# Differential attention on one core: where the heads' small PE work stands between the projection's half units, and how the second softmax map is scaled

## The reference

```
q, k = rmsnorm(q) * 64**-0.5, rmsnorm(k)             # per head two maps of 64 values
s    = einsum('bqhtd,bkhtd->bhtqk', q, k) + bias     # t = 0, 1: the two maps
pr   = softmax(s)                                    # over 512 keys
attn = pr[:, :, 0] - lam * pr[:, :, 1]
o    = rmsnorm(attn @ v) * (1 - lam_init)            # per head, 128 values, eps 1e-6
o    = o * silu(z);  out = o @ w_out
```

## Time and profile before

| what | value |
|---|---|
| median of three runs | 821.05 us |
| the profiled execution: time, span | 821.67 us, 819.9 us |
| PE busy in the span | 764.7 us, 93% |
| DVE, ACT, POOL busy | 503.3, 402.1, 451.8 us |
| chain that ended last | PE 49%, DVE 23%, issue 12%, ACT 7%, POOL 7% |
| head iterations 0 to 10 and the end | 488.7 to 819.9 us of the span |

### The profile page before, as it was taken

How to read it: one execution, slowest core, us unless ns; L and a number is a source line. 1 busy time by engine, 2 the same in 40 slices (tenths; PEclk the granted TensorE clock), 3 DMA queues, 4 the chain that set the end, 5 groups by cost and what they waited for, 6 DMA issues and landing times.

```text
span 819.9 us, 11592 instructions
## 1 busy us (share of the span) xinstructions
PE 764.7 (93%) x3856; PEld 616.5 (75%) x3856; DVE 503.3 (61%) x880; ACT 402.1 (49%) x806; POOL 451.8 (55%) x258
## 2 busy tenths in 40 slices
PE   4999999999999999997999999989999999998788
PEld 3777788878878787875878887767777777776566
DVE  4756858585848576773841131566867768678632
ACT  6447473728283745555531244264545554654510
POOL 5457574848484857564845326654553735536101
PEclk9999999999999999998999999999999999999898
DMA  8274464644637263534532224322313222220002
GB/s 252 79 217 103 160 148 154 155 155 111 198 76 206 76 167 114 154 155 102 180 105 84 78 77 126 114 70 68 100 53 100 74 76 75 69 82 26 0 1 102
DMA packets 100196, 91.10 MB, mean 111 GB/s; under 512 B 5456, under 2 KB 87728, under 8 KB 97080
## 3 DMA queue, kind: packets, MB, share of 16 engines
q1 hardware_dynamic: 95760, 66.99, 27.9%
q10 hardware_dynamic: 4264, 23.50, 9.4%
q0 software_dynamic: 128, 0.05, 0.0%
HBM read 88.13 MB, written 2.39 MB: 110 GB/s over the span
## 4 chain that ended last, share of the span: by engine, by line
PE 49%; DVE 23%; issue 12%; ACT 7%; POOL 7%; DMA 1%; DVEq 1%; ACTq 0%; SPq 0%; POOLq 0%
PE bank L1343 42%; DVE c_acc L995 6%; POOL w_lo L486 3%; DVE bank L1089 2%; ACT ex L835 2%; POOL stat L477 2%; PE bank L1420 2%; DVE sbias L1210 2%; DVE bank L1081 1%; DVE ex L1221 1%; ACT qkvz L900 1%; DVE tmp L1076 1%; ACT w_hi L621 1%; DVE stat L1214 1%; PE bank L1394 1%
## 5 line engine op out<-in xcount | busy, mean ns | idle before, releaser
L486 POOL TENSOR_TENSOR w_lo<-w_raw,w_hi 128x1024 fp32r<-128x1024 f32 x104 | 257.8, 2481 | 229.2 <-ACT w_hi L621 229.1
L1343 PE MATMUL bank<-hn_hi,w_hi 128*128 128x512 f32 (+1 forms) x392 | 157.3, 401 | 14.7 <-DVE BT L1010 11.7
L1343 PE MATMUL bank<-hn_hi,w_lo 128*128 128x512 f32 (+1 forms) x392 | 153.2, 391 | 0.0
L1343 PE MATMUL bank<-hn_lo,w_hi 128*128 128x512 f32 (+1 forms) x392 | 152.8, 390 | 0.0
L621 ACT CAST w_hi<-w_raw 128x1024 fp32r<-128x1024 f32 x104 | 108.7, 1047 | 72.1 <-PE bank L1343 68.4
L1343 PE MATMUL bank<-w_hi,hn_hi 128*128 128x512 f32 x320 | 131.4, 411 | 8.8 <-DVE zT L1010 6.1
L1343 PE MATMUL bank<-w_lo,hn_hi 128*128 128x512 f32 x320 | 125.9, 393 | 0.0
L1343 PE MATMUL bank<-w_hi,hn_lo 128*128 128x512 f32 x320 | 125.8, 393 | 0.0
L995 DVE SCALAR_TENSOR_TENSOR c_acc<-bank,par,c_acc 128x510 f32<-128x510 f32 (+1 forms) x128 | 95.8, 749 | 26.0 <-ACT c_acc L665 17.2
L835 ACT ACTIVATE ex<-sbias,stat 128x512 f32<-128x512 f32 x64 | 45.7, 716 | 120.5 <-DVE stat L1214 120.5
L1343 PEld LDWEIGHTS bank<-hn_hi,w_hi 128*128 128x128 f32 (+1 forms) x392 | 73.2, 187 | 33.1 <-issue 15.6
(11 more groups left out here) (191 smaller groups left out, 1231.9 us busy)
## 6 DMA issues: line engine op xcount, KB each, us to landing
w_raw<-in_ssd_w_in SPq DMA_DIRECT2D x48, 512.0 KB, 4.1
w_raw<-in_attn_w_in SPq DMA_DIRECT2D x64, 256.0 KB, 3.1
rows<-acs_rows ACTq DMA_DIRECT2D x14, 1024.0 KB, 6.0
edec<-exp_rows ACTq DMA_DIRECT2D x16, 512.0 KB, 6.3
w_raw<-in_ssd_w_out SPq DMA_DIRECT2D x16, 512.0 KB, 3.6
w_raw<-in_attn_w_out SPq DMA_DIRECT2D x16, 256.0 KB, 3.1
wbias<-bias_rows SPq DMA_DIRECT2D x8, 448.0 KB, 4.2
rows<-in_x SPq DMA_DIRECT2D x4, 512.0 KB, 5.2
```

The costliest lines, as they stand in the source:

```text
L486: nc.gpsimd.tensor_tensor(w_lo[:, s, :], w_raw[:, s, :], f32(w_hi[:, s, :]), ALU.subtract)\
L1343: ins = T.matmul(dst, a[i], b[j], start=first and n == 0, stop=last and n == 2)
```

## The change

The head steps of iterations 0 to 10 are put in another order on every engine, and one instruction changes its size:

- **PE.** Behind the even-numbered half units (the second, fourth, sixth and eighth, that is s = 1, 3, 5, 7) stand scores first, then the output's transposes or the values, then the transposes of the probabilities. Block 2 goes from s = 0 to 1, block 3 from 2 to 3, block 0 from 4 to 5, block 1 from 6 to 7. The transposes of q and k go from s = 3, where they stood ahead of `probs_t`, to s = 4, alone. Stages 0, 2 and 6 have no head step. In iterations 8 and 9 the fills go to (8; 1, 3, 4, 5, 7) and (9; 1).
- **ACT.** `exps` follow the scores to stages 1, 3, 5 and 7. In stage 1 and 3 `probs_hi` stands ahead of `exps`; in stage 5 the output's split and `probs_hi` do. In stage 7 the evacuation of the next head stands ahead of `exps`. v and z go from stage 1 to 2, the split of q and k from 3 to 4, behind that stage's `split_hi`.
- **DVE.** In the same manner; `biased` of block 1 and `combine` of block 1 both stand in stage 7, the gate in stage 6, the squares' reduction of the output in stage 3, its scaling in stage 4.
- **POOL.** The small `power` of the output goes from stage 2 (ahead of v's low part) to stage 3.
- **Arithmetic.** `combine` no longer divides map 0 by its sum: it works out one number per row, -lam times sum 0 over sum 1, and adds map 1 times that to map 0. The head's output is thereby larger by sum 0, and the RMS norm's epsilon is multiplied by the square of sum 0 (one more small instruction for each head). The 128x512 instruction L1221 becomes a 128x1 one.

Instructions of the PE, the exponentials, the transfers and all other sizes stay. Of the orders, the diff shows the lines as they stand after the change; those taken away stand in the listing above.

```diff
@@ -577,10 +578,10 @@
             pool.wait_ge(qk_ms, it)
             power(stat[:, 16:32], stat[:, 0:16], 4 * NC).then_inc(qk_rs, 1)
     par_ = (half + 1) % 2
+    if s == 3 and has(3):
+        pool.wait_ge(o_ms, it - 2)
+        power(stat[:, 52:56], stat[:, 48:52], NC).then_inc(o_rs, 1)
     if s == 2:
-        if has(3):
-            pool.wait_ge(o_ms, it - 2)
-            power(stat[:, 52:56], stat[:, 48:52], NC).then_inc(o_rs, 1)
...
@@ -827,13 +828,14 @@
 nc.scalar.activation(stat[:, 60:62], stat[:, 60:62], ACT.Exp).then_inc(sp_a, 1)
 act.wait_ge(h_rstd, 1)
-def exps(hd, q):
+def exps(hd, q, par_):
     act.wait_ge(smax, hd * NC + q + 1)
     after(act, a_done, hd * NC + q)
     for j in range(2):
+        total = SUM0 + par_ * NC + q if j == 0 else 41
         nc.scalar.activation(ex[:, j, :], sbias[:, j, :], ACT.Exp, bias=stat[:, 36 + j:37 + j],
-                             accum_out=stat[:, 40 + j:41 + j]).then_inc(e_done, 1)
+                             accum_out=stat[:, total:total + 1]).then_inc(e_done, 1)
...
@@ -843,64 +845,59 @@
 def stage_ops(m, half, s, has):
     it = m * 2 + 2 + half
+    one, two = (half + 1) % 2, half
+    if s == 0 and has(3):
+        act.wait_ge(pv_done, it - 2)
+        after(act, og_done, it - 3)
+        nc.scalar.copy(o_chan[:, :], bank[7][:, :]).then_inc(o_copied, 1)
+    if s == 1 and has(2):
+        probs_hi(it - 2, 1)
+        exps(it - 2, 2, two)
+    if s == 2:
         if has(1):
             act.wait_ge(qkvz_in, it * NC)
             after(act, pv_done, it - 2)
+            nc.scalar.copy(v_hi[:, one, :, :], qkvz[:, :, 2 * SEG:3 * SEG]).then_inc(v_hi_done, 1)
             after(act, gate_done, it - 1)
             nc.scalar.activation(ztan[:, :, :], qkvz[:, :, 3 * SEG:4 * SEG], ACT.Tanh, scale=0.5)\
                 .then_inc(ztan_done, 1)
         if has(3):
             act.wait_ge(o_back, it - 2)
             nc.scalar.activation(o_chan[:, :], bank[7][:, :], ACT.Square).then_inc(o_sqd, 1)
+    if s == 3 and has(2):
+        probs_hi(it - 2, 2)
+        exps(it - 2, 3, two)
     if s == 4 and has(1):
+        for j in range(2):
+            act.wait_ge(tqk_done, (it - 1) * 2 + j + 1)
+            after(act, s_done, (it - 1) * 2 * NC)
+            if j == 0:
+                nc.scalar.activation(qT_hi[:, 0, :], bank[4][:, :], ACT.Copy, scale=chan[:, 3:4])\
+                    .then_inc(qk_hi, 1)
+            else:
+                nc.scalar.copy(qT_hi[:, 1, :], bank[5][:, :]).then_inc(qk_hi, 1)
     if s == 5:
         if has(3):
             act.wait_ge(ot_done, it - 2)
             nc.scalar.activation(oT_hi_flat[:, ds((it - 3) * L, L)], bank[7][:, :], ACT.Copy,
                                  scale=chan[:, 2:3]).then_inc(ot_hi, 1)
+        if has(2):
+            probs_hi(it - 2, 3)
+        if has(1):
+            exps(it - 1, 0, one)
+    if s == 7:
+        if has(0):
+            act.wait_ge(unit_done, it * UPH + (U_AT + UPH))
+            after(act, tqk_done, it * 2)
+            after(act, v_lo_done, it)
+            after(act, gate_done, it)
+            for c in range(NC):
+                nc.scalar.activation(qkvz[:, c, :], bank[c][:, :], ACT.Copy,
+                                     scale=small[:, 36 + c:37 + c]).then_inc(qkvz_in, 1)
+        if has(1):
+            exps(it - 1, 1, one)
+            probs_hi(it - 1, 0)
...
@@ -1213,14 +1210,15 @@
     own(ins)
     V.tensor_scalar(stat[:, 36:38], stat[:, 32:34], -1.0, None, ALU.mult).then_inc(smax, 1)
-def combine(hd, q):
+def combine(hd, q, par_):
     dve.wait_ge(e_done, (hd * NC + q) * 2 + 2)
     after(dve, t_done, hd * NC + q - 1)
-    own(V.reciprocal(stat[:, 44:46], stat[:, 40:42]))
-    own(V.tensor_scalar(ex[:, 1, :], ex[:, 1, :], stat[:, 45:46], lam, ALU.mult, ALU.mult))
-    V.scalar_tensor_tensor(am[:, q % 2, :], ex[:, 0, :], stat[:, 44:45], ex[:, 1, :],
-                           ALU.mult, ALU.subtract).then_inc(a_done, 1)
+    total = stat[:, SUM0 + par_ * NC + q:SUM0 + par_ * NC + q + 1]
+    own(V.reciprocal(stat[:, 45:46], stat[:, 41:42]))
+    own(V.tensor_scalar(stat[:, 46:47], stat[:, 45:46], total, neg_lam, ALU.mult, ALU.mult))
+    V.scalar_tensor_tensor(am[:, q % 2, :], ex[:, 1, :], stat[:, 46:47], ex[:, 0, :],
+                           ALU.mult, ALU.add).then_inc(a_done, 1)
...
@@ -1229,36 +1227,39 @@
 def stage_ops(m, half, s, has):
     it = m * 2 + 2 + half
+    one, two = (half + 1) % 2, half
+    if s == 0 and has(1):
+        dve.wait_ge(qk_sqd, it)
+        own(V.reduce_sum(stat[:, 64:80], qk_sq[:, :, :].rearrange("p c (s n) -> p (c s) n", n=HD),
+                         axis=AXX))
+        V.tensor_scalar(stat[:, 0:16], stat[:, 64:80], 1.0 / HD, EPS, ALU.mult, ALU.add)\
+            .then_inc(qk_ms, 1)
+    if s == 1 and has(2):
+        biased(it - 2, 2, two)
+        probs_lo(it - 2, 1)
+    if s == 2:
         if has(1):
             qk = qkvz[:, :, 0:2 * SEG].rearrange("p c (s n) -> p c s n", n=HD)
             dve.wait_ge(qk_rs, it)
             dve.wait_ge(qkvz_in, it * NC)
             V.tensor_tensor(qk, qk, stat[:, 16:32].rearrange("p (c s) -> p c s", c=NC)
                             .unsqueeze(3).to_broadcast([P, NC, 4, HD]), ALU.mult).then_inc(qk_ready, 1)
         if has(2):
+            combine(it - 2, 2, two)
+    if s == 3:
+        if has(2):
+            biased(it - 2, 3, two)
+            probs_lo(it - 2, 2)
         if has(3):
+            total = stat[:, SUM0 + one * NC:SUM0 + (one + 1) * NC]
+            V.scalar_tensor_tensor(stat[:, 88:92], total, EPS, total, ALU.mult, ALU.mult)
             dve.wait_ge(o_sqd, it - 2)
             own(V.reduce_sum(stat[:, 56:60], o_sq[:, :, :], axis=AXX))
+            V.scalar_tensor_tensor(stat[:, 48:52], stat[:, 56:60], 1.0 / SEG, stat[:, 88:92],
+                                   ALU.mult, ALU.add).then_inc(o_ms, 1)
+    if s == 4:
         if has(2):
+            combine(it - 2, 3, two)
         if has(1):
             for j in range(2):
                 dve.wait_ge(qk_hi, (it - 1) * 2 + j + 1)
@@ -1268,41 +1269,33 @@
                 else:
                     V.tensor_tensor(qT_lo[:, 1, :], bank[5][:, :], f32(qT_hi[:, 1, :]),
                                     ALU.subtract).then_inc(qk_lo, 1)
         if has(3):
             dve.wait_ge(o_rs, it - 2)
             after(dve, ot_done, it - 3)
             for c in range(NC):
                 ins = V.scalar_tensor_tensor(o_nat[:, c, :], bank[7][:, c * SEG:(c + 1) * SEG],
+                                             stat[:, 52 + c:53 + c], gate[:, one, c, :],
                                              ALU.mult, ALU.mult)
             ins.then_inc(og_done, 1)
     if s == 5:
         if has(1):
+            biased(it - 1, 0, one)
         if has(3):
             dve.wait_ge(ot_hi, it - 2)
             V.scalar_tensor_tensor(oT_lo_flat[:, ds((it - 3) * L, L)], bank[7][:, :], chan[:, 2:3],
                                    f32(oT_hi_flat[:, ds((it - 3) * L, L)]),
                                    ALU.mult, ALU.subtract).then_inc(ot_lo, 1)
+        if has(2):
+            probs_lo(it - 2, 3)
+    if s == 6 and has(1):
+        dve.wait_ge(ztan_done, it)
+        V.scalar_tensor_tensor(gate[:, one, :, :], ztan[:, :, :], 1.0, qkvz[:, :, 3 * SEG:4 * SEG],
+                               ALU.add, ALU.mult).then_inc(gate_done, 1)
+        combine(it - 1, 0, one)
     if s == 7 and has(1):
+        biased(it - 1, 1, one)
+        combine(it - 1, 1, one)
         probs_lo(it - 1, 0)
...
@@ -1570,47 +1563,53 @@
                       (aT_hi[:, c, :], aT_lo[:, c, :]), c == 0, c == NC - 1)
     ins.then_inc(pv_done, 1)
+def o_natural(hd):
+    pe.wait_ge(o_copied, hd + 1)
+    for c in range(NC):
+        ins = T.transpose(bank[7][:, c * P:(c + 1) * P], o_chan[:, c * P:(c + 1) * P], ident[:, :])
+    ins.then_inc(o_back, 1)
+def o_channels(hd):
+    pe.wait_ge(og_done, hd + 1)
+    for c in range(NC):
+        ins = T.transpose(bank[7][:, c * P:(c + 1) * P], o_nat[:, c, :], ident[:, :])
+    ins.then_inc(ot_done, 1)
+def qk_channels(hd):
+    pe.wait_ge(qk_ready, hd + 1)
+    after(pe, smax, hd * NC)
+    for j in range(2):
+        for c in range(NC):
+            ins = T.transpose(bank[4 + j][:, c * P:(c + 1) * P],
+                              qkvz[:, c, j * SEG:(j + 1) * SEG], ident[:, :])
+        ins.then_inc(tqk_done, 1)
 def stage_ops(m, half, s, has):
     it = m * 2 + 2 + half
+    if s == 1:
         if has(2):
+            scores(it - 2, 2)
+        if has(3):
+            o_natural(it - 3)
+        if has(2):
+            probs_t(it - 2, 1)
+    if s == 3 and has(2):
+        scores(it - 2, 3)
+        probs_t(it - 2, 2)
+    if s == 4 and has(1):
+        qk_channels(it - 1)
+    if s == 5:
         if has(1):
+            scores(it - 1, 0)
+        if has(3):
+            o_channels(it - 3)
         if has(2):
+            probs_t(it - 2, 3)
     if s == 7:
+        if has(1):
+            scores(it - 1, 1)
         if has(2):
```

(84 more changed lines are left out.)

61 lines of the change are left out of this document (7 added, 54 removed).

## The result

The changed kernel takes 811.99 us (median of 4 runs, 811.74 to 812.16), the kernel before on the same chip 820.86 (820.36 to 821.7): a ratio of 0.989 (95% interval 0.987 to 0.990). Forecast were 811.1 us and faster. In a later set the same kernel took 808.56 (5 runs, 806.16 to 811.29), ratio 0.985 (0.983 to 0.987); its nine runs spread over 6 us, and why is a part of what follows. The profiled execution took 812.08 us, span 810.3.

A forecast was written before the change was run, and what follows sets the result against it. The PE was taken as the bound, busy 32.7 of 33.3 us per steady iteration. Removed 21.3 us, added 11.4, net 9.9 off 821.67 gives 811.8; the median lies 0.6 lower, 811.1, range 806.5 to 817.5.

The forecast's parts named there:

- the forecast case: The expected outcome for the whole kernel: faster, 811.1 us, given a chance of 0.65.
- signs of being wrong: DVE's `am` held in steady iterations, a granted clock below 1.0 before iteration 8, or iterations over 33 us.
- The drain's new waits: Iterations 8 and 9: new PE waits at `probs_t`, scores of block 3, `probs_t` and before `out2`, 6.8 us together.
- Iteration 2: PE waits for block 2's `combine` result near 545 us: a new wait of 0.5 to 2.0 us, 1.3 taken.
- at worst: In iteration 2 `combine` meets `v_lo` (1.3 us) besides POOL's weight split; the result comes between 545.6 and 547.0.
- The packing: PE's new order of scores, transposes and products saves 0.1 us an iteration, 0.8 in all; by the tiling-mode rule alone, nothing.
- 0.5 beside the small waits: Iterations 3 to 7: 0.08 us beside each small listed wait for `qT_lo` goes too, 0.5 in the sum.
- Waits removed: Between 500 and 820 us, 14.9 of 18.5 us of listed PE waits go; new ones of 1.3 and 6.8 come.
- Clock: PE's low-clock spells behind waits in iterations 8, 9 and the end: three go (5.1 us), two come (3.3 us).
- nothing waits for that: In steady state `combine` gets 0.4 us shorter, and nothing waits for its result.

The follow-up runs named there:

- e1: The kernel before, in its old order, with only the new arithmetic of the probabilities: 819.21 us, ratio 0.997.
- e2: The changed kernel, in its new order, with the old arithmetic (128x512 scaling of the second map): 812.71 us, ratio 0.988.
- e7: The changed kernel run again with nothing altered, in a later set: 808.56 us, ratio 0.985.
- e3: The changed kernel with one 128x512 memset added on VectorE ahead of block 3's combination: 821.39 us, ratio 0.999.
- e6: The changed kernel with 24 idle transposes in TensorE's 6.05 us wait at 378.6 us; the stretch from the first product to the next wait took 10.41 us.
- e10: The changed kernel with more idle transposes in more waits (16, 97, 378.6 us, iterations 8 and 9): 806.69 us, ratio 0.979.
- e8: The changed kernel with idle transposes in three places (16.3 us, 378.6 us, iteration 9): median 804.57 us.

## Why the prediction was right, and by which steps not

The direction and the forecast case were right, and so were its places: no wait for `qT_lo`, iteration 1 of 25.3 us (531.5 - 506.2 forecast, 25.30 measured), a new wait in iteration 2, values of the last heads without a wait, `am` held in two places. That 811.1 lay 0.9 us from the result is luck in part: the sum was 4.8 us short in the heads, and the part ahead of them was 5.1 us longer. One of its signs of being wrong, a granted clock below 1.0 before iteration 8, did appear, but only ahead of the heads (18, 100 and 384 us), where before too it was low (378 us). By its terms:

- **The drain's new waits**: 2.1, 0.9, 1.8, 2.0 forecast; 1.68, 0.86, 1.79, 1.58 measured, 5.9 in place of 6.8. Laying out each queue from known durations did this.
- **Iteration 2**: 1.3 taken (0.5 to 2.0); 0.39 measured. `combine` met the weight split as said and was held by it, but `v_lo` came behind `combine`. That `v_lo` would hold it too was the step's "at worst", and a value half way there had been taken:

```profile
547.54 2.43 POOL L487 TENSOR_TENSOR w_lo<-w_raw,w_hi 128x1024 fp32r<-128x1024 f32 x1 [1.08 <-ACT w_hi L622]
...
548.14 2.39 DVE L1220 SCALAR_TENSOR_TENSOR am<-ex,stat 128x512 f32<-128x512 f32 x1
...
549.93 1.75 POOL L588 TENSOR_TENSOR v_lo<-qkvz,v_hi 128x512 fp32r<-128x512 f32 x1
```

- **The packing**: this term was half of what it should be. 0.1 us an iteration was forecast. e1, whose order is the old one, has 32.87 us with 0.19 of delay at the scores of block 0 (0.51 from the product ahead to them, against 0.32 at the three others), so 32.68; the new order has 32.48 (162.41 over five) in four profiles: 0.20. The rest that no wait explains is more than forecast as well: of the heads' 14.7 us, waits are 8.6 (18.5 - 9.9), clock 3.4 (8.5 lost before, 5.1 after), and 2.7 are left, where 0.8 of packing and 0.5 beside the small waits were counted. What makes the new order 0.20 cheaper was not taken apart. That the packing gives nothing, which the prediction drew from the Trainium skill ("TensorEngine Tiling (Array Packing)", Key Properties: a change of the tiling mode drains the array), was not borne out by the 0.20.
- **Waits removed** net of new ones: 6.8 forecast (14.9 - 8.1), 8.6 measured.
- **Clock**: 1.8 forecast (three spells go, two come), 3.4 measured. Three went and two came, as counted; the third portion gained stood behind the last output, which the prediction left as it was (3.4 us from 797 us on before, 1.7 from 790 on after). The second profile lost one portion less still, so no term of this kind can be forecast for one run.
- **Left out**: that the part before the heads can differ by 5 us between executions of the same kernel (511.30 and 506.41). Against the second set (808.56) the forecast is 2.5 us slow, on the side on which its sum fell short.
- The arithmetic was treated as a detail in the steady state ("nothing waits for that"). True there, since e2's steady iterations are as long; but e2 lacks 2.9 us of the heads' gain, in iteration 2, iteration 8 and the drain.

## What to carry to other kernels

When the PE bounds a loop, lay out each queue between two of its needs from measured durations and look at the margins: here 0.9 us on the PE's side and 0.4 us ahead of a collision, and half a microsecond of harmless work in each iteration cost ten in all. Move work so that an evacuation starts the moment its unit ends, with other PE work behind it. And before a change of 1% is explained, run the same kernel again: the part that the change does not touch tells how much of the difference is chance.

## What the runs showed of the hardware

- The granted clock fell to 0.50 in portions worth 1.7 us. In the profiles before and after they stood at waits of 1.6 to 2.6 us and at one of 6.06 us (two portions), at places that differ between executions of the same kernel: the wait of 1.92 us at 99 us had one in the changed kernel, the same wait (1.90) none in e7. Waits of 1.45 us once in 34 us (e3) brought none. The Trainium skill ("TensorE: Matmul & The Clock Gate", Part 1: The HAM clock gate) says that the slow stretch of a start varies from run to run; these runs show the same in mid kernel, worth 0.7% of the time.
- Transposes that nobody reads, put into a wait, cost nothing where they end before the awaited event: 24 took 2.6 of 6.06 us, and the wait ended as long after the work ahead of it as without them. They went with a higher clock behind the wait in some profiles (e6, e10), not in all (e8).
- VectorE's factor of one element a row (L1219) took 271 to 275 ns in 32 executions, also when `w_lo` was under way (at 547.83 in iteration 2), while `am` right behind it was held for 1.6 us.
